# One transformer layer with retrieved experts: gate products copied by ScalarE and multiplied in by GpSimd

## The chip, the core and the metric

One core of a Trainium2 chip. The metric is the device time of one execution in microseconds, the median of three runs. The engines are named as in the profile: PE is TensorE (matmuls; PEld its weight loads), DVE is VectorE, ACT is ScalarE, POOL is GpSimd, SP is SyncE, which only issues transfers here.

## What is computed

One encoder layer on 512 tokens of width 1024 in float32. Its first half (a projection, a gating group, a retention group, an output projection, a layer norm) is not touched. Its second half retrieves experts:

```
q = h @ w_q;  scores = q . sub_keys             # 8 heads, 2 x 128 keys
top_s, top_i = top_k(scores, 16)                # per half of the query
cand = top_s[0][:, None] + top_s[1][None, :]    # 256 pairs, expert = i0 * 128 + i1
best, expert_idx = top_k(cand, 16);  gates = softmax(best)
act = gelu(h . u_tab[expert_idx])               # 128 experts a token
ffn = sum(gates * act * v_tab[expert_idx])
out = layer_norm(2 ** 0.25 * h + ffn)
```

## The kernel before

The 512 tokens are four tiles of 128. Tiles 0 and 1 are *gathered*: for each of 256 rows (16 units of a tile and a head, 16 experts each) GpSimd issues an indirect DMA for a row of `u_tab` and, 32 rows later (`LAG`), one for the row of `v_tab`; VectorE forms the dot product (`product_row`, L916) and adds the weighted row to the tile's sum (`add_row`, L937). Each kind has a ring of six buffers, so a gather waits until VectorE has used the row six before. VectorE's program is one loop over n = 0 to 287, in which the choices of later units (`choose_gathered`, `choose_dense`) stand at fixed rows.

Tiles 2 and 3 are *dense*: all 16384 experts are computed for their 256 tokens by TensorE, in two rounds of 64 blocks of 128 experts. A round has three parts in TensorE's order (`static_jobs`): `act`, products with 64 blocks of `u_tab`, whose GELU ScalarE writes to `X` (partitions are experts of a block, 64 blocks x 256 tokens); `gate`, which turns the chosen indices into dense weights; `expert`, products of the weighted `X` with 64 blocks of `v_tab`, accumulated in PSUM banks 0 to 3. SyncE loads the 256 blocks in this order into a ring of eight buffers (`load_block`, L440); block b waits until block b - 8 is used.

The gate part has 32 groups (`GROUPS`) of 8 tokens a round. For each, VectorE compares the tokens' second and first key indices with a grid, which gives one-hots in bf16 (`eqi`, L953, for 64 of the first keys; `ohj`, L954, for the 128 second keys), multiplies the first by the gates split in three bf16 pieces (`ohi`, L959), and TensorE multiplies the two (24 matmuls, L1264) into a PSUM bank of 8 tokens x 64 blocks. VectorE then multiplies that bank into `X` (`dense_weights`, L982) for the group before the one whose one-hots it just made. `ohi` has one buffer, `ohj` two. The banks rotate over four. The rounds stand in VectorE's loop in front of row 70 and row 190, with all 32 groups at once; TensorE's experts wait for `s_wgtd`, which VectorE signals at a round's end.

Tile 0's last norm (`finish`, `layer_norm`, L671 to L679) stands at row 160; its weights `lnp2` lie over the scores of tile 0 and are loaded by SyncE between block 127 and block 128, once eight units are chosen. Tile 1's norm follows row 287, then those of the dense tiles. SBUF is nearly full: `S` (first 8192 columns of `pool_mem`) holds the scores of all tiles, 2048 columns each, and `X` covers the rest and the scores of the dense tiles.

Of the kernel before, what the change touches and what calls it, by code (L numbers as in the profile page):

```python
# [5 lines left out]
P = 128  # L6
# [5 lines left out]
PH, TOPK, NK = 8, 16, 128  # L12
RING = 6
# [4 lines left out]
HALF = NK // 2  # L18
# [5 lines left out]
ROUND_ROW = (70, 190)  # L24
PER_ROW = 32

# [28 lines left out]
def static_jobs():  # L55
# [6 lines left out]
    def add(kind, *arg, by):  # L62
        jobs.append((kind, arg, by))
# [87 lines left out]
    for r in range(2):  # L151
        for n in range(HALF // 2):
            add("act", r, n, by="act")
            if (r, n) in during:
                jobs.append(("gelu", (during[r, n],), None))
            if (r, n) == (0, 28):
                jobs.append(("gates", (), None))
        if r == 0:
            add("selT", 0, by="act")
            add("selT", 1, by="act")  # L160
        for n in range(GROUPS):
            add("gate", r, n, by="dve")
            if (r, n) in within:
                jobs.append(("gelu", (within[r, n],), None))
        for u in range(4, 7) if r == 0 else range(10, GUNITS):
            jobs.append(("gelu", (u,), None))
        for n in range(HALF):
            jobs.append(("expert", (r, n), None))
# [29 lines left out]
def layer(nc, x, w_in, sgu_ln_w, sgu_ln_b, sgu_w_s, sgu_b, decay_fwd, decay_bwd, gn_w, w_out, ln1_w, ln1_b,  # L198
# [12 lines left out]
    with ctx:  # L211
# [48 lines left out]
        X = pool_mem[:, 4096:20480].rearrange("p (i n) -> p i n", i=HALF)  # L260
        lnp2 = S[:, 0:2048].rearrange("p (a n) -> p a n", a=2)
        S4 = S.rearrange("p (t q n) -> p t q n", t=NT, q=2 * PH)
# [26 lines left out]
        lookd = y[:, 3072:4096].bitcast(bf16)  # L289
        ohi = sb("ohi", [P, 2, 3, HALF, 4], bf16)  # L290
        grid = sb("grid", [P, NK, 4], bf16)
        table = sb("table", [P, TOPK, TOPK], bf16)
        work = sb("work", [P, 512])
        lookg = work[:, 0:256].bitcast(bf16)
        eqi = work[:, 256:512].bitcast(bf16).rearrange("p (q n t) -> p q n t", q=2, t=4)
        ident = sb("ident", [P, P])
# [64 lines left out]
        s_oh = sem("onehots_ready")  # L361
        s_act, s_wgtd = sem("dense_gelu_ready"), sem("dense_weights_ready")
        s_vdone = sem("experts_added")
# [18 lines left out]
        def _(sp):  # L382
# [58 lines left out]

            for b in range(2 * HALF):
                load_block(b)
            sp.wait_ge(s_best, PH)
            sp.dma_start(lnp2[:, 0, :], ln2_w[0].partition_broadcast(P)).then_inc(s_ln, 16)
            sp.dma_start(lnp2[:, 1, :], ln2_b[0].partition_broadcast(P)).then_inc(s_ln, 16)
            for b in range(2 * HALF, 4 * HALF):
                load_block(b)
# [9 lines left out]
        def _(pool):  # L458
# [36 lines left out]
            def gather_v(n):  # L495
# [3 lines left out]
                if n >= RING:  # L499
# [3 lines left out]
                                             ).then_inc(s_v[n % RING], 16)  # L503

            for n in range(ROWS + LAG):
                if n < ROWS:
                    gather_u(n)
                if n >= LAG:
                    gather_v(n - LAG)
# [3 lines left out]
        def _(act):  # L513
# [12 lines left out]
            for kind, arg, by, b, n in JOBS:  # L526
# [93 lines left out]
                elif kind == "selT":  # L620
                    a = arg[0]
                    copy(selT[:, 0:2, a * P:(a + 1) * P], bank4[:, 0:2, :])
                    copy(gateT[0][:, a * P:(a + 1) * P], bank4[:, 2, :]).then_inc(free[b], 1)
                    A.drain().then_inc(s_selT, 1)

            for t in range(GATHERED):
# [7 lines left out]
        def _(dve):  # L634
# [294 lines left out]
            def add_row(n):  # L929
# [9 lines left out]
                fence()  # L939

            def gate_rows(r, n):

                g = r * GROUPS + n
                t0 = 8 * n

                def spread(row, width):
                    return selT[:, row, t0:t0 + 8].rearrange("p (q t) -> p q t", q=2).unsqueeze(2).broadcast_to(
                        [P, 2, width, 4])

                def both(part, width):  # L950
                    return part.unsqueeze(1).broadcast_to([P, 2, width, 4])

                V.tensor_tensor(eqi, spread(0, HALF), both(grid[:, r * HALF:(r + 1) * HALF, :], HALF), ALU.is_equal)  # L953
                V.tensor_tensor(ohj[:, g % 2], spread(1, NK), both(grid[:], NK), ALU.is_equal)  # L954
                fence()
                if g:
                    b, used_ = BANK["gate", (g - 1) // GROUPS, (g - 1) % GROUPS]
                    dve.wait_ge(full[b], used_ + 1)
                V.tensor_tensor(ohi[:].rearrange("p q c n t -> p q c (n t)"),  # L959
                                eqi.rearrange("p q n t -> p q (n t)").unsqueeze(2).broadcast_to([P, 2, 3, HALF * 4]),  # L960
                                pieces[:, 2 * n:2 * n + 2].rearrange("p q c t -> p (q c) t").unsqueeze(2).broadcast_to(
                                    [P, 6, HALF, 4]), ALU.mult)
                fence().then_inc(s_oh, 1)  # L963

            def gate_pieces():

                for c in range(3):
# [6 lines left out]
                    fence()  # L974

            def dense_weights(r, n):
                b, used_ = BANK["gate", r, n]
                dve.wait_ge(full[b], used_ + 1)
                if n == 0:
                    dve.wait_ge(s_act, r + 1)  # L980
                x3 = X[:, :, 8 * n:8 * n + 8]
                V.tensor_tensor(x3, ps[:, b, :].rearrange("p (t i) -> p i t", t=8), x3, ALU.mult).then_inc(free[b], 1)  # L982

# [22 lines left out]
            for n in range(ROWS + LAG):  # L1006
# [9 lines left out]
                for r in range(2):  # L1016
                    if n == ROUND_ROW[0] and r == 0:
                        dve.wait_ge(s_selT, 2)
                        gate_pieces()
                    if 0 <= n - ROUND_ROW[r] < GROUPS // PER_ROW:  # L1020
                        first = (n - ROUND_ROW[r]) * PER_ROW
                        for g in range(first, first + PER_ROW):
                            gate_rows(r, g)
                            if g:
                                dense_weights(r, g - 1)
                        if first + PER_ROW == GROUPS:
                            dense_weights(r, GROUPS - 1)
                            fence().then_inc(s_wgtd, 1)  # L1028
                if n < ROWS:
                    product_row(n)  # L1030
                if n >= LAG:
                    add_row(n - LAG)
                if n == PH * TOPK + LAG:
                    dve.wait_ge(s_ln, 64)
                    finish(acc_rows[0]).then_inc(s_ln2, 1)
                    fence()
# [15 lines left out]
        def _(pe):  # L1052
# [43 lines left out]
            for kind, arg, by, b, n in JOBS:  # L1096
                if kind in ("split", "norm", "scale", "gelu", "gates"):
                    continue
                if kind == "expert":
                    r, i = arg  # L1100
                    if i == 0:
                        pe.wait_ge(s_wgtd, r + 1)
                    if i == 0 and r == 0:
# [154 lines left out]
                elif kind == "gate":  # L1258
# [3 lines left out]
                    for t in range(8):  # L1262
                        for c in range(3):
                            last = T.matmul(bank[:, t * HALF:(t + 1) * HALF], ohj[:, g % 2, t // 4, :, t % 4],  # L1264
                                            ohi[:, t // 4, c, :, t % 4],
                                            start=(c == 0), stop=(c == 2))
# [43 lines left out]
```

## Time and profile before

| | us |
|---|---|
| median of three runs (1617.83 to 1618.03) | 1617.87 |
| the profiled execution, its own time | 1619.71 |
| its span in the profile | 1617.6 |

| engine | busy, us | share of the span |
|---|---|---|
| TensorE matmul | 1398.0 | 86% |
| VectorE | 1226.6 | 76% |
| GpSimd | 631.8 | 39% |
| ScalarE | 175.1 | 11% |

A row of the profile names the line of the kernel, the engine, the operation and what it writes and reads, `out<-in`. "Idle before" is the time in which the engine stood still just before it, with what ended that wait. Busy shares are means over stages with different limits; the stages are, in order: the first half of the layer to about 240 us, queries and scores to 390, then round 0 (acts, gates, experts) and round 1 (the same), with the gathered rows beside them, and a tail of gathered rows and norms.

### The profile page before, as it was taken

To read this page: it belongs to the slowest core of one execution; us is meant where nothing else is said; L and a number is where in the kernel's file an instruction comes from. 1 tells how busy PE (TensorE), PEld (TensorE's weight loads), DVE (VectorE), ACT (ScalarE), POOL (GpSimd) and SP (SyncE) were. 2 spreads that over 40 slices of the span, in tenths; PEclk is the share of its full clock that TensorE was granted. 3 is DMA by queue.
4 is the path that set the end of the run, shared out by engine and by line. 5 is a ranking of instruction groups with operands and counts; after the bars stand their busy time and mean duration, and the time that the engine had idled before them with its cause. 6 is when DMAs were issued, how large, how long until landed. Compare 5 with 4: busy or idle time off the path is not lost.

```text
span 1617.6 us, 18280 instructions
## 1 busy us (share of the span) xinstructions
PE 1398.0 (86%) x6410; PEld 964.5 (60%) x6410; DVE 1226.6 (76%) x2527; ACT 175.1 (11%) x272; POOL 631.8 (39%) x548
## 2 busy tenths in 40 slices
PE   8999989999999999558999999999995599999600
PEld 6787655888777777454444457777775544444200
DVE  5745527788889883899867758778878987856888
ACT  4223001112110102000000001101011000000000
POOL 2243101222334262004636455664660046544671
PEclk9999999999999999557999999999995589999855
DMA  6320513465988799005999999999992069999993
GB/s 233 119 89 16 208 52 130 157 203 208 387 316 304 286 369 343 4 1 218 409 409 409 409 409 409 409 409 380 410 409 116 1 244 409 410 409 409 410 329 131
DMA packets 136714, 444.24 MB, mean 275 GB/s; under 512 B 13616, under 2 KB 26416, under 8 KB 136624
## 3 DMA queue, kind: packets, MB, share of 16 engines
q0 software_dynamic: 73728, 268.47, 42.9%
q1 hardware_dynamic: 62320, 173.56, 28.4%
q8 instruction: 51, 0.84, 0.2%
q10 hardware_dynamic: 576, 1.05, 0.2%
q14 instruction: 39, 0.32, 0.1%
HBM read 440.93 MB, written 2.10 MB: 274 GB/s over the span
## 4 chain that ended last, share of the span: by engine, by line
PE 40%; DMA 25%; DVE 17%; POOL 9%; issue 6%; DVEq 2%; ACT 1%; ACTq 0%; SPq 0%; POOLq 0%
PE ps L1057 23%; DMA big<-in_peer_v_dram,idx 22%; PE ps L1264 7%; PE ps L1074 6%; POOL big L501 5%; POOL big L491 4%; DVE ohi L959 4%; DVE y L937 3%; DMA big<-in_peer_u_dram,idx 2%; DVE big L916 2%; PE ps L1215 1%; PE ps L1242 1%; PE ps L1196 1%; DVE nw L661 1%; PE ps L1170 1%
## 5 line engine op out<-in xcount | busy, mean ns | idle before, releaser
L491 POOL DMA_INDIRECT big<-in_peer_u_dram,idx x256 | 289.0, 1129 | 683.5 <-DVE dots L916 565.0
L916 DVE CUSTOM_DVE_ANT_0 big<-big,xh 128x1024 f32<-128x1024 f32 x256 | 312.0, 1225 | 92.2 <-DMA big<-in_peer_u_dram,idx 73.5
L937 DVE SCALAR_TENSOR_TENSOR y<-big,wgt,y 128x1024 f32<-128x1024 f32 x256 | 328.5, 1283 | 69.0 <-DMA big<-in_peer_v_dram,idx 65.9
L501 POOL DMA_INDIRECT big<-in_peer_v_dram,idx x256 | 281.8, 1101 | 129.9 <-DVE y L937 69.2
L1057 PE MATMUL ps<-xT,big 128*128 128x256 f32 x1024 | 237.1, 385 | 10.8 <-issue 8.3
L1057 PEld LDWEIGHTS ps<-xT,big 128*128 128x128 f32 x1024 | 189.5, 190 | 58.5 <-issue 35.5
L1109 PE MATMUL ps<-big,pool_mem 128*128 128x512 f32 x512 | 222.3, 592 | 0.0
L1264 PE MATMUL ps<-ohi,y 128*128 128x64 bf16 x1536 | 105.7, 242 | 80.0 <-DVEq L963 80.0
L1109 PEld LDWEIGHTS ps<-big,pool_mem 128*128 128x128 f32 x512 | 97.4, 190 | 122.3 <-issue 122.3
L1264 PEld LDWEIGHTS ps<-ohi,y 128*128 128x128 bf16 x1536 | 96.5, 125 | 89.4 <-issue 89.4
L1057 PE MATMUL ps<-xT 128*128 128x256 f32 x512 | 118.5, 385 | 5.4 <-issue 4.1
L1109 PE MATMUL ps<-xT,pool_mem 128*128 128x512 f32 x256 | 112.5, 592 | 0.0
L1057 PEld LDWEIGHTS ps<-xT 128*128 128x128 f32 x512 | 94.7, 190 | 29.2 <-issue 17.7
L1057 PE MATMUL ps<-xT,pool_mem 128*128 128x256 f32 (+1 forms) x512 | 101.5, 358 | 1.8 <-ACTq L588 1.5
L1057 PEld LDWEIGHTS ps<-xT,pool_mem 128*128 128x128 f32 x512 | 87.3, 193 | 12.0 <-issue 2.4
L616 ACT ACTIVATE pool_mem<-ps 128x512 f32<-128x512 f32 x64 | 38.2, 597 | 498.3 <-PE ps L1057 498.3
L1109 PEld LDWEIGHTS ps<-xT,pool_mem 128*128 128x128 f32 x256 | 48.7, 190 | 61.2 <-issue 61.2
L1074 PE MATMUL ps<-weight_parts,x_hi 128*128 128x512 f32 x320 | 82.8, 404 | 0.8 <-ACT weight_parts L517 0.8
L375 POOL TENSOR_TENSOR weight_parts<-big,weight_parts 128x1024 fp32r<-128x1024 f32 x20 | 49.0, 2473 | 84.4 <-ACT weight_parts L517 84.4
L1074 PEld LDWEIGHTS ps<-weight_parts,x_hi 128*128 128x128 f32 x320 | 59.8, 191 | 14.7 <-ACT weight_parts L517 2.4
L959 DVE TENSOR_TENSOR ohi<-work,pieces 128x1536 bf16<-128x1536 bf16 x64 | 61.3, 958 | 9.4 <-PE ps L1264 2.3
L1109 PE MATMUL ps<-wr,pool_mem 128*128 128x512 f32 x128 | 61.7, 628 | 1.7 <-DVEq L1028 1.7
(193 smaller groups left out, 1425.3 us busy)
## 6 DMA issues: line engine op xcount, KB each, us to landing
big<-u_blocks_dram SPq DMA_DIRECT2D x64, 512.0 KB, 7.0
big<-in_peer_v_dram SPq DMA_DIRECT2D x64, 512.0 KB, 6.8
xT<-u_blocks_dram SPq DMA_DIRECT2D x32, 512.0 KB, 6.8
xT<-in_peer_v_dram SPq DMA_DIRECT2D x32, 512.0 KB, 6.8
big<-in_w_in_dram SPq DMA_DIRECT2D x24, 512.0 KB, 5.7
pool_mem<-in_peer_w_q_dram SPq DMA_DIRECT2D x12, 1024.0 KB, 5.5
wr<-u_blocks_dram SPq DMA_DIRECT2D x16, 512.0 KB, 6.9
y<-u_blocks_dram SPq DMA_DIRECT2D x16, 512.0 KB, 6.8
```

The source lines that it names most:

```text
L375: return engine.tensor_tensor(w_lo(g)[:, ks, :], w_full(g)[:, ks, :], w_hi(g)[:, ks, :].bitcast(f32), ALU.subtract)
L491: nc.gpsimd.indirect_dma_start(urow[n % RING], None, peer_u2, bass.IndirectOffsetOnAxis(ap=idx[:, u, e:e + 1], axis=0)).then_inc(s_u[n % R ...
L501: nc.gpsimd.indirect_dma_start(vrow[n % RING], None, peer_v2, bass.IndirectOffsetOnAxis(ap=idx[:, u, e:e + 1], axis=0)).then_inc(s_v[n % R ...
L616: A.activation(X[:, i:i + 2, :], bank.rearrange("p (i n) -> p i n", i=2), ACT.Gelu).then_inc(free[b], 1)
L661: V.scalar_tensor_tensor(r, a, 1.5, r, ALU.add, ALU.mult)
L916: V.tensor_tensor_reduce(out=urow[n % RING], in0=urow[n % RING], in1=xh[:, u // PH * D:(u // PH + 1) * D], scale=1.0, scalar=0.0, op0=ALU. ...
L937: V.scalar_tensor_tensor(acc_rows[t], vrow[n % RING], wgt[:, u % 2, e:e + 1], acc_rows[t], ALU.mult, ALU.add).then_inc(s_vadd, 1)
L959: V.tensor_tensor(ohi[:].rearrange("p q c n t -> p q c (n t)"), eqi.rearrange("p q n t -> p q (n t)").unsqueeze(2).broadcast_to([P, 2, 3, ...
L1057: last = T.matmul(dst, lhs(i), rhs(i), start=(i == 0), stop=(i == n - 1))
L1074: last = T.matmul(dst, *((a, b_) if x_left else (b_, a)), start=(n == 0 and k == 0), stop=(n == 2 and k == KC - 1))
L1109: last = T.matmul(acc[a][:, half * 512:(half + 1) * 512], X[:, i, a * P:(a + 1) * P], rows_v[:, half * 512:(half + 1) * 512], start=(r == ...
L1264: last = T.matmul(bank[:, t * HALF:(t + 1) * HALF], ohj[:, g % 2, t // 4, :, t % 4], ohi[:, t // 4, c, :, t % 4], start=(c == 0), stop=(c ...
```

## The change

- A gate job's bank is now read by ScalarE, which copies it with its two inner axes exchanged into `gbuf` (two buffers of 512 columns in tile 0's part of `S`), frees the bank and signals `s_gbuf`. From the third copy on it waits for the product two before.
- GpSimd multiplies `gbuf` into `X` (`dense_weights`, now in GpSimd's program, 32 at once in front of its gathers n = 76 and n = 196) and signals `s_prod`, for which TensorE's experts now wait.
- VectorE no longer multiplies. It makes `eqi` one group ahead (`first_key`, two buffers), `ohi` has a second buffer, and it waits for the matmuls of the group before last instead of the last; the drain between `ohj` and `ohi` is gone.
- `lnp2` moves to tile 1's part of `S`. Its two loads stand in front of block 240 and wait for all 16 units' choices; tile 0's norm stands at row 240.

```
--- before.py
+++ after.py
@@ -22,7 +22,8 @@
-PER_ROW = 32
+LN2_BLOCK = 240
+FINISH0 = 240
...
@@ -159,7 +160,7 @@
-            add("gate", r, n, by="dve")
+            add("gate", r, n, by="act")
...
@@ -258,7 +259,8 @@
-        lnp2 = S[:, 0:2048].rearrange("p (a n) -> p a n", a=2)
+        gbuf = [S[:, 512 * k:512 * k + 512].rearrange("p (i t) -> p i t", t=8) for k in range(2)]
+        lnp2 = S[:, 2048:4096].rearrange("p (a n) -> p a n", a=2)
...
@@ -287,12 +289,14 @@
-        ohi = sb("ohi", [P, 2, 3, HALF, 4], bf16)
+        ohi = [half.bitcast(bf16).rearrange("p (q c n t) -> p q c n t", q=2, c=3, t=4)
+               for half in (sb("ohi", [P, 768])[:, :], S[:, 1024:1792])]
...
-        eqi = work[:, 256:512].bitcast(bf16).rearrange("p (q n t) -> p q n t", q=2, t=4)
+        eqi = [work[:, 256 * k:256 * k + 256].bitcast(bf16).rearrange("p (q n t) -> p q n t", q=2, t=4)
+               for k in range(2)]
...
@@ -439,12 +443,12 @@
-            for b in range(2 * HALF):
+            for b in range(LN2_BLOCK):
                 load_block(b)
-            sp.wait_ge(s_best, PH)
+            sp.wait_ge(s_best, GUNITS)
             sp.dma_start(lnp2[:, 0, :], ln2_w[0].partition_broadcast(P)).then_inc(s_ln, 16)
             sp.dma_start(lnp2[:, 1, :], ln2_b[0].partition_broadcast(P)).then_inc(s_ln, 16)
-            for b in range(2 * HALF, 4 * HALF):
+            for b in range(LN2_BLOCK, 4 * HALF):
                 load_block(b)
...
@@ -502,7 +506,19 @@
+            def dense_weights(r):
+
+                pool.wait_ge(s_act, r + 1)
+                for n in range(GROUPS):
+                    g = r * GROUPS + n
+                    pool.wait_ge(s_gbuf, g + 1)
+                    x3 = X[:, :, 8 * n:8 * n + 8]
+                    nc.gpsimd.tensor_tensor(x3, gbuf[g % 2], x3, ALU.mult).then_inc(s_prod, 1)
+
             for n in range(ROWS + LAG):
+                for r in range(2):
+                    if n == ROUND_ROW[r] + RING:
+                        dense_weights(r)
                 if n < ROWS:
                     gather_u(n)
...
@@ -622,6 +638,13 @@
+                elif kind == "gate":
+                    r, n_ = arg
+                    g = r * GROUPS + n_
+                    if g >= 2:
+                        act.wait_ge(s_prod, g - 1)
+                    copy(gbuf[g % 2], bank.rearrange("p (t i) -> p i t", t=8)).then_inc(free[b], 1)
+                    A.drain().then_inc(s_gbuf, 1)
...
@@ -938,26 +961,30 @@
+            def first_key(r, n):
+
+                V.tensor_tensor(eqi[n % 2], spread(0, n, HALF), both(grid[:, r * HALF:(r + 1) * HALF, :], HALF),
+                                ALU.is_equal)
+
             def gate_rows(r, n):
 
                 g = r * GROUPS + n
...
-                V.tensor_tensor(eqi, spread(0, HALF), both(grid[:, r * HALF:(r + 1) * HALF, :], HALF), ALU.is_equal)
-                V.tensor_tensor(ohj[:, g % 2], spread(1, NK), both(grid[:], NK), ALU.is_equal)
-                fence()
-                if g:
-                    b, used_ = BANK["gate", (g - 1) // GROUPS, (g - 1) % GROUPS]
+                if n + 1 < GROUPS:
+                    first_key(r, n + 1)
+                if g >= 2:
+                    b, used_ = BANK["gate", (g - 2) // GROUPS, (g - 2) % GROUPS]
                     dve.wait_ge(full[b], used_ + 1)
-                V.tensor_tensor(ohi[:].rearrange("p q c n t -> p q c (n t)"),
-                                eqi.rearrange("p q n t -> p q (n t)").unsqueeze(2).broadcast_to([P, 2, 3, HALF * 4]),
+                V.tensor_tensor(ohj[:, g % 2], spread(1, n, NK), both(grid[:], NK), ALU.is_equal)
+                V.tensor_tensor(ohi[g % 2].rearrange("p q c n t -> p q c (n t)"),
+                                eqi[n % 2].rearrange("p q n t -> p q (n t)").unsqueeze(2).broadcast_to(
+                                    [P, 2, 3, HALF * 4]),
                                 pieces[:, 2 * n:2 * n + 2].rearrange("p q c t -> p (q c) t").unsqueeze(2).broadcast_to(
                                     [P, 6, HALF, 4]), ALU.mult)
                 fence().then_inc(s_oh, 1)
...
@@ -972,14 +999,6 @@
-            def dense_weights(r, n):
-                b, used_ = BANK["gate", r, n]
-                dve.wait_ge(full[b], used_ + 1)
-                if n == 0:
-                    dve.wait_ge(s_act, r + 1)
-                x3 = X[:, :, 8 * n:8 * n + 8]
-                V.tensor_tensor(x3, ps[:, b, :].rearrange("p (t i) -> p i t", t=8), x3, ALU.mult).then_inc(free[b], 1)
...
@@ -1017,20 +1036,16 @@
-                    if 0 <= n - ROUND_ROW[r] < GROUPS // PER_ROW:
-                        first = (n - ROUND_ROW[r]) * PER_ROW
-                        for g in range(first, first + PER_ROW):
+                    if n == ROUND_ROW[r]:
+                        first_key(r, 0)
+                        fence()
+                        for g in range(GROUPS):
                             gate_rows(r, g)
-                            if g:
-                                dense_weights(r, g - 1)
-                        if first + PER_ROW == GROUPS:
-                            dense_weights(r, GROUPS - 1)
-                            fence().then_inc(s_wgtd, 1)
                 if n < ROWS:
                     product_row(n)
                 if n >= LAG:
                     add_row(n - LAG)
-                if n == PH * TOPK + LAG:
+                if n == FINISH0:
                     dve.wait_ge(s_ln, 64)
                     finish(acc_rows[0]).then_inc(s_ln2, 1)
                     fence()
...
@@ -1099,7 +1114,7 @@
                     if i == 0:
-                        pe.wait_ge(s_wgtd, r + 1)
+                        pe.wait_ge(s_prod, GROUPS * (r + 1))
...
@@ -1262,7 +1277,7 @@
                             last = T.matmul(bank[:, t * HALF:(t + 1) * HALF], ohj[:, g % 2, t // 4, :, t % 4],
-                                            ohi[:, t // 4, c, :, t % 4],
+                                            ohi[g % 2][:, t // 4, c, :, t % 4],
```

## Rows read from the trace of the kernel before

**Rows 1.** Page: the chain's shares by engine; the DMA rate in 40 slices.
```profile
PE 40%; DMA 25%; DVE 17%; POOL 9%; issue 6%; DVEq 2%; ACT 1%; ACTq 0%; SPq 0%; POOLq 0%
GB/s 233 119 89 16 208 52 130 157 203 208 387 316 304 286 369 343 4 1 218 409 409 409 409 409 409 409 409 380 410 409 116 1 244 409 410 409 409 410 329 131
```

**Rows 2.** Windows: stretch, length, busy of PE, PEld, DVE, ACT, POOL, PEclk, DMA share, GB/s.
```profile
1250.00:1300.00 50.00, 29.01 (x424) 26.42 (x421) 45.73 (x71) 0.00 (x0) 0.00 (x0) 0.50 0.00 1
...
1460.00:1500.00 40.00, 40.00 (x95) 17.71 (x94) 24.93 (x29) 3.18 (x5) 18.52 (x20) 1.00 1.03 409
...
1510.00:1524.00 14.00, 14.00 (x34) 5.95 (x32) 13.21 (x17) 0.00 (x0) 10.65 (x12) 1.00 1.03 410
```

**Rows 3.** Timeline, one step of round 0: start, us, engine, line, tiles [idle before].
```profile
658.22 0.96 DVE L959 TENSOR_TENSOR ohi<-work,pieces 128x1536 bf16<-128x1536 bf16 x1
659.29 0.69 DVE L982 TENSOR_TENSOR pool_mem<-ps,pool_mem 128x512 f32<-128x512 f32 x1
...
659.35 1.66 PE L1264 MATMUL ps<-ohi,y 128*128 128x64 bf16 x24 [1.17 <-DVEq L963]
659.90 0.41 DVE L953 TENSOR_TENSOR work<-selT,grid 128x512 bf16<-128x512 bf16 x1
660.23 0.68 DVE L954 TENSOR_TENSOR y<-selT,grid 128x1024 bf16<-128x1024 bf16 x1
661.05 0.96 DVE L959 TENSOR_TENSOR ohi<-work,pieces 128x1536 bf16<-128x1536 bf16 x1
```

**Rows 4.** Timeline, 148 to 151 us: a ScalarE copy, GpSimd, VectorE beside it.
```profile
148.56 0.60 ACT L580 ACTIVATE pool_mem<-ps 128x512 f32<-128x512 f32 x1 [3.94 <-PE ps L1074]
149.34 1.27 POOL L477 TENSOR_TENSOR pool_mem<-pool_mem 128x512 f32<-128x512 f32 x1 [13.35 <-ACTq L581]
149.42 0.69 DVE L798 SCALAR_TENSOR_TENSOR big<-ps,y 128x512 f32<-128x512 f32 x1 [5.33 <-PE ps L1170]
```

**Rows 5.** Timeline, VectorE beside GpSimd's multiplications, and the same forms alone.
```profile
30.29 2.28 DVE L726 TENSOR_TENSOR dec<-dec 128x8 f32<-128x8 f32 x1
...
54.64 2.81 DVE L677 SCALAR_TENSOR_TENSOR pool_mem<-pool_mem,mv 128x512 f32<-128x512 f32 x1
57.52 0.75 DVE L679 SCALAR_TENSOR_TENSOR pool_mem<-pool_mem,nw 128x512 f32<-128x512 f32 x1
...
118.87 0.17 DVE L694 TENSOR_TENSOR dec<-dec 128x8 f32<-128x8 f32 x1
...
124.90 2.40 POOL L375 TENSOR_TENSOR weight_parts<-big,weight_parts 128x1024 fp32r<-128x1024 f32 x1 [7.83 <-ACT weight_parts L517]
127.87 3.12 DVE L715 SCALAR_TENSOR_TENSOR y<-pool_mem,dec,y 128x896 f32<-128x896 f32 x1
...
137.80 1.15 DVE L715 SCALAR_TENSOR_TENSOR y<-pool_mem,dec,y 128x896 f32<-128x896 f32 x1
...
198.81 1.53 DVE L987 CAST grid<-iota 128x512 bf16<-128x512 f32 x1
```

**Rows 6.** Timeline, end of round 0 and begin of round 1.
```profile
738.74 1.64 PE L1264 MATMUL ps<-ohi,y 128*128 128x64 bf16 x24 [1.17 <-DVEq L963]
741.21 6.08 PE L1109 MATMUL ps<-wr,pool_mem 128*128 128x512 f32 x8 [0.83 <-DVEq L1028]
742.78 1.74 POOL L491 DMA_INDIRECT big<-in_peer_u_dram,idx  x1 [108.43 <-DVE dots L916]
...
1212.30 1.64 PE L1264 MATMUL ps<-ohi,y 128*128 128x64 bf16 x24 [1.31 <-DVEq L963]
```

**Rows 7.** Landing of L445 and L446; timeline: row 241; tile 1's norm, first, last.
```profile
DMA to landing us min/median/max: 10.2/11.3/12.3
...
1502.91 1.23 DVE L916 CUSTOM_DVE_ANT_0 big<-big,xh 128x1024 f32<-128x1024 f32 x1 [0.95 <-DMA big<-in_peer_u_dram,idx]
...
1590.68 1.29 DVE L671 BATCH_NORM_STATS2 st<-y 128x6 f32<-128x512 f32 x2
...
1596.99 0.75 DVE L679 SCALAR_TENSOR_TENSOR y<-y,nw,pool_mem 128x512 f32<-128x512 f32 x1
```

More of the change, by code:

```diff
@@ L361, in layer @@
         s_oh = sem("onehots_ready")
-        s_act, s_wgtd = sem("dense_gelu_ready"), sem("dense_weights_ready")
+        s_act, s_gbuf, s_prod = sem("dense_gelu_ready"), sem("gate_products_copied"), sem("dense_weights_ready")
         s_vdone = sem("experts_added")
@@ L939, in add_row, with both, spread @@
                 fence()
+            def both(part, width):
+                return part.unsqueeze(1).broadcast_to([P, 2, width, 4])
+            def spread(row, n, width):
+                return selT[:, row, 8 * n:8 * n + 8].rearrange("p (q t) -> p q t", q=2).unsqueeze(2).broadcast_to(
+                    [P, 2, width, 4])
+            def first_key(r, n):
+                V.tensor_tensor(eqi[n % 2], spread(0, n, HALF), both(grid[:, r * HALF:(r + 1) * HALF, :], HALF),
+                                ALU.is_equal)
             def gate_rows(r, n):
                 g = r * GROUPS + n
[L944 to L951, printed above, removed]
-                V.tensor_tensor(eqi, spread(0, HALF), both(grid[:, r * HALF:(r + 1) * HALF, :], HALF), ALU.is_equal)
-                V.tensor_tensor(ohj[:, g % 2], spread(1, NK), both(grid[:], NK), ALU.is_equal)
-                fence()
-                if g:
-                    b, used_ = BANK["gate", (g - 1) // GROUPS, (g - 1) % GROUPS]
+                if n + 1 < GROUPS:
+                    first_key(r, n + 1)
+                if g >= 2:
+                    b, used_ = BANK["gate", (g - 2) // GROUPS, (g - 2) % GROUPS]
                     dve.wait_ge(full[b], used_ + 1)
-                V.tensor_tensor(ohi[:].rearrange("p q c n t -> p q c (n t)"),
-                                eqi.rearrange("p q n t -> p q (n t)").unsqueeze(2).broadcast_to([P, 2, 3, HALF * 4]),
+                V.tensor_tensor(ohj[:, g % 2], spread(1, n, NK), both(grid[:], NK), ALU.is_equal)
+                V.tensor_tensor(ohi[g % 2].rearrange("p q c n t -> p q c (n t)"),
+                                eqi[n % 2].rearrange("p q n t -> p q (n t)").unsqueeze(2).broadcast_to(
+                                    [P, 2, 3, HALF * 4]),
                                 pieces[:, 2 * n:2 * n + 2].rearrange("p q c t -> p (q c) t").unsqueeze(2).broadcast_to(
```

## Prediction

> **What bounds the kernel now.** I read the chain of work that ended last first. It names TensorE, the DMA of gathered rows, VectorE and GpSimd in turn [rows 1], so no engine is the limit everywhere, and the question is which one ends each stage. The slices show two holes in the DMA traffic [rows 1]. These are the two gate rounds, 32 groups each, about 646 to 741 us and 1210 to 1302 us. The table of windows shows what such a stretch is like and what the others are like: inside round 1 the DMA queues carry nothing, the granted clock is 0.50 and VectorE is busy 91% of the time. In the expert phase the DMA is saturated at 409 GB/s, TensorE is busy without a gap and VectorE waits. In the last stretch before TensorE ends, VectorE is busy 13.21 of 14 us [rows 2].
>
> One step of a gate round is in [rows 3]. VectorE makes the first one-hot (0.42 us), the second (0.68), the gated one (0.96), then multiplies a finished gate out of PSUM (0.69). The gated one-hot starts at 658.22 and again at 661.05, so a step takes 2.83 us, and nothing on that engine waits. TensorE needs 1.66 us of each step and idles for the rest, waiting for the one-hots. A round is therefore VectorE's serial time, and nothing else advances in it. Each microsecond per step is 64 us of the kernel.
>
> **The step without its multiplication.** By starts in [rows 3], first to second one-hot is 0.33 us, second to gated 0.82, gated to multiplication 1.07, multiplication to the next first one-hot 0.61. The change removes the last interval. It also takes away the drain between second and gated one-hot: there 0.60 remains (0.68 less the 0.08 that consecutive instructions overlap). Sum: 0.33 + 0.60 + 1.07 = 2.00 us. TensorE still needs 1.66 us plus the 0.17 us from the end of the gated one-hot to its first matmul [rows 3], so 1.83, under 2.00. With two gated buffers its wait for the group before last is past. ScalarE copies 128x512 out of PSUM in 0.60 us, and GpSimd starts 0.78 us after such a copy starts [rows 4]. The reads here are strided by 64 elements; VectorE reads this layout in the 0.69 us that it also takes for a straight one [rows 3, 4], so I take no surcharge and bound it at twice the copy, which would still be under a step. GpSimd multiplies 128x512 by 128x512 in 1.27 us [rows 4]. So each of the four engines alone would fit in 2.00 us.
>
> **What GpSimd's multiplication does to VectorE.** Three rows decide this. A VectorE instruction of 8 elements with two SBUF inputs takes 0.17 us alone, and 2.28 us when it begins under a GpSimd multiplication. A cast to bf16 of 512 elements takes 1.53 us beside GpSimd's. Yet one that reads PSUM and only one SBUF tensor takes its usual 0.69 us in the middle of GpSimd's 1.27 [rows 4, 5]. The multiplication that is removed was of the last kind; the three one-hot instructions that stay read two SBUF tensors each. The price comes from a stretch in which both engines had work queued: VectorE's instruction of line 715, 1.15 us alone, took 3.12 us there, so the 1024-wide GpSimd operation, 2.40 us long, put 1.97 us into VectorE's sequence: its length less 0.43 [rows 5]. For 512 elements this gives 1.27 - 0.43 = 0.84 us. A second place shows a smaller overlap: a 512-wide instruction, 0.75 us alone, took 2.81 us, so 2.06 us were put in, the length less 0.34 [rows 5]; that gives 0.93. I take 0.90. Bounds: nothing (step 2.00) and the whole 1.27 (step 3.27). I stay near 0.90 since both direct rows lie there.
>
> The step then is 2.00 + 0.90 = 2.90 us against 2.83: the gain of 0.83 is eaten and 0.07 us is lost. Does GpSimd come at the cheap place? A product is ready 0.17 + 1.66 + 0.04 + 0.78 = 2.65 us after the end of its gated one-hot; the next gated one-hot runs from 1.94 to 2.90 on that scale. So GpSimd waits for its end and takes the gap at the drain, as in the priced stretch. If it came between the second and the gated one-hot, which have no drain between them, it would put in some 0.2 us more per step, 13 us in all.
>
> The Trainium skill (SBUF — State Buffer, Who interferes with whom) says that a VectorE instruction with two SBUF inputs contends with a GpSimd instruction that reads SBUF, that the two share ports under an exclusive lock, and that the loser is blocked for the whole instruction. The trace agrees on who is blocked (2.28 against 0.17 us), but not quite on the amount: by the page the step would be the plain sum 3.27 us and the kernel some 24 us slower than by my step, which I keep as an end of the range.
>
> **The edges of the rounds.** Entry to round 0 is set by TensorE and ScalarE; the first group now makes one more first one-hot and a drain before TensorE can start: 0.4 us. In each round the first step has no GpSimd product yet (-0.9) and the second product may fall at the dearer place (+0.2). So round 0 costs VectorE 0.4 + 31 x 0.07 - 0.7 = 1.9 us. At its end, TensorE started the experts 0.83 us after its last gate matmul [rows 6]. Now ScalarE (0.04 + 0.78) and GpSimd (1.27) and a semaphore (0.1) stand there: 2.2 us, or up to 3.4 where VectorE's next row instruction, which also reads two SBUF tensors (1.23 us [rows 7]), goes first. That is 1.4 to 2.6; I take 2.0. TensorE leaves round 0 3.9 us late and works without a gap up to round 1. There it had waited 1.31 us for the first one-hots [rows 6]. VectorE reaches that point earlier relative to it now, since a norm and two loads have left the stretch (below), so 1.2 of it are given back: round 1 starts 2.7 us late. It takes +1.5, rows start again with two products still to go on GpSimd, in front of its gathers: before, the first gather was issued 742.78, 2.4 us after TensorE's last gate (740.38) [rows 6], now some 3.3: +0.9, partly covered by the six rows that lie ready. I book 0.5. Rows run 4.7 us late.
>
> On ScalarE the gelus of the next units now stand behind the copies; they are first needed two rows after a round, 5 us away, and I cost them at nothing. GpSimd's gathers behind the products wait for rows that VectorE has not yet used, so they lose only the 0.5 above.
>
> **The late norm.** The tile-0 norm takes 7.1 us of VectorE (1590.68 to 1597.74 for the same work on tile 1 [rows 7]). At row 160 it lay in the saturated stretch, where VectorE waits for rows. At row 240 it lies at about 1502 us: the row before it came with 0.95 us of waiting [rows 7], the ones after 1506 with none, VectorE being 94% busy [rows 2]. So little absorbs it: 1.3 us of row waits directly, up to 3 if the saturated stretch lasts longer because TensorE is late. Cost 4 to 6; I take 5. If all were absorbed it would be nothing, at worst 7.1.
>
> The two loads of the norm's weights (0.5 MB each into 128 partitions) move from before round 1, where TensorE sets the end, to before block 240, where the row chain is short of bandwidth: 1.05 MB / 409 GB/s = 2.6 us [rows 2]. They landed within 12.3 us of issue [rows 7]. On SyncE's queue they now wait for unit 15's choice, made at row 210; SyncE reaches block 240 when expert 40 of round 1 is used, at about 1303 + 40 x 3.4 = 1439 us (95 matmul records in 40 us [rows 2], 8 to a block). Row 210 comes at about 1382 (row 190 at 1303, row 241 at 1502.91 [rows 7]: 3.9 us each). So that wait is past, eight blocks are loaded ahead, and row 240 comes 50 us after the loads. No stall.
>
> **Sum.** 4.7 + 2.6 + 5 = 12.3 us on a span of 1617.6. The profiled execution took 1619.71 us, 2.1 around the span; the median is 1617.87, so the profile is 0.1% slow and the difference carries over. 1617.9 + 12.3 = 1630 us.
>
> **Rivals.** (a) GpSimd does not block the bf16 one-hots (no row shows bf16 instructions with two inputs beside it). Then a step is 2.00 us: 1630 less 62 x 0.90 = 1574. For it: only that the exact form is unseen. Against it: every two-input row beside GpSimd, and the bf16 cast. 11%. (b) Partial blocking, 0.2 to 0.7 us per step: 1587 to 1618. 9%. (c) The other side, and my forecast: the products put 0.8 to 1.1 us into each step: 1624 to 1642. It decides from 0.70 us per step on, where 62 x (0.83 - 0.70) = 8 us of gain just pay for the other 8 us of the sum (edges, loads and norm, 12.3 - 62 x 0.07). 65%. (d) GpSimd's product is dearer than 1.27, because it reads and writes runs of 8 elements 1 KB apart, or nothing overlaps: 3.1 to 3.6 us a step, 1642 to 1673. Its straight and its 128-element-run forms differ by nothing that matters; runs of 8 are unseen. 15%.
>
> **How the numbers follow.** About 0.2% (3 us) is what a measurement of this kernel tells from no change. Likeliest: (c), 1630. Its own range is 1624 to 1642. The range to 8 in 10 takes (c), the upper half of (b) and most of (d): 1602 to 1655. Slower by over 0.2%: (c) nearly whole, (d): 0.79. Same: the edge between (b) and (c), 0.04. Faster: 0.17.
>
> **What would show it.** In the profile after: the distance of successive gated one-hots, 2.9 us (2.0 means (a)); the mean of VectorE's bf16 instructions in a round, one of the three longer by 0.9 to 1.2 us per step; GpSimd's 64 products at 1.3 to 2.2 us; TensorE waiting about 1.2 us per step for one-hots at clock 0.50; the norm at row 240 and no row waits after it; experts starting 2.2 to 3.4 us after the last gate matmul. I am wrong if the bf16 forms run at 0.42, 0.68 and 0.96 beside GpSimd, or if the product's layout is slow.

## The result, and the profile after

| | before, us | after, us |
|---|---|---|
| median (4 runs each) | 1617.95 | 1629.19 |
| lowest to highest | 1617.83 to 1621.08 | 1627.99 to 1630.44 |
| profiled execution: its time, its span | 1619.71, 1617.6 | 1629.49, 1627.7 |

The changed kernel is slower, by a ratio of 1.0065 (95% interval 1.005 to 1.0079). The forecast was 1630, with "slower by over 0.2%" at 0.79.

Timeline of the changed kernel, one step of round 0 and the start of the next (start, us, engine, line, tiles, idle before); it answers [rows 3]. L973 is the first one-hot, L984 the second, L985 the gated one, L533 ScalarE's copy, L516 GpSimd's product:

```profile
658.96 1.31 DVE L973 TENSOR_TENSOR work<-selT,grid 128x512 bf16<-128x512 bf16 x1
659.02 1.65 PE L1279 MATMUL ps<-pool_mem,y 128*128 128x64 bf16 x24 [1.26 <-DVEq L990]
660.20 0.68 DVE L984 TENSOR_TENSOR y<-selT,grid 128x1024 bf16<-128x1024 bf16 x1
660.71 0.60 ACT L533 ACTIVATE pool_mem<-ps 128x512 f32<-128x512 f32 x1 [2.32 <-PE ps L1279]
660.80 0.94 DVE L985 TENSOR_TENSOR ohi<-work,pieces 128x1536 bf16<-128x1536 bf16 x1
661.42 1.48 POOL L516 TENSOR_TENSOR pool_mem<-pool_mem 128x512 f32<-128x512 f32 x1 [1.43 <-ACTq L647]
661.86 1.31 DVE L973 TENSOR_TENSOR work<-selT,grid 128x512 bf16<-128x512 bf16 x1
```

The first one-hot starts at 658.96 and at 661.86: a step is 2.90 us, where 2.83 was before. The multiplication is gone from VectorE, and the first one-hot, 0.42 us before, takes 1.31. It begins 0.11 us after the gated one-hot ends and lasts to 663.17, 0.27 us past the end of GpSimd's product at 662.90. GpSimd's own row begins at 661.42, under the gated one-hot, which is not lengthened: there GpSimd is the one that waits. TensorE works 1.65 us and waits 1.26.

Windows of the changed kernel, busy us of PE, PEld, DVE, ACT, POOL, then granted clock, DMA share, GB/s; they answer [rows 2]:

```profile
1250.00:1300.00 50.00, 28.34 (x413) 25.74 (x410) 47.98 (x53) 10.42 (x18) 25.31 (x17) 0.50 0.01 1
1460.00:1500.00 40.00, 40.00 (x94) 17.68 (x93) 22.89 (x28) 0.00 (x0) 16.86 (x18) 1.00 1.03 409
```

In the round ScalarE and GpSimd now work too, yet VectorE's busy time rose from 45.73 to 47.98 of 50 us, because blocked time counts as busy. The granted clock is 0.50 in both kernels, the lower of TensorE's two levels (1.2 GHz). In the saturated stretch TensorE is busy without a gap and the DMA at 409 GB/s, as before.

**Where the 10.1 us of span came from.** By starts of the same instruction in the two timelines (after less before):

| instruction | shift, us |
|---|---|
| gated one-hot of group 0, round 0 | +0.15 |
| gated one-hot of group 31, round 0 | +1.3 |
| first expert matmul, round 0 | +3.4 |
| first gate matmul, round 1 | +2.4 |
| gated one-hot of group 31, round 1 | +3.4 |
| row 190, row 192 | +0.8, +2.7 |
| row 240 (both weight loads lie in front) | +5.7 |
| row 241 (the norm lies in front) | +12.3 |
| last added row, its end; end of the span | +10.1 |

### The profile page after: what moved, and what is told of

Its sections match the earlier page's. It is cut to its first block, busy times and chain, and to the rows that moved or that the text cites. A ratio compares the mean times of both kernels' runs of the same rounds, so it can differ in the third digit from the quotient of the medians.

```text
span 1627.7 us, 18406 instructions
## 1 busy us (share of the span) xinstructions
PE 1398.6 (86%) x6410; PEld 964.6 (59%) x6410; DVE 1241.4 (76%) x2463; ACT 213.4 (13%) x336; POOL 738.4 (45%) x612
## 4 chain that ended last, share of the span: by engine, by line
PE 62%; DVE 17%; DMA 8%; issue 4%; POOL 4%; DVEq 4%; ACT 1%; ACTq 0%; SPq 0%
PE ps L1072 37%; PE ps L1124 14%; DMA big<-in_peer_v_dram,idx 8%; PE ps L1089 6%; DVE work L973 5%; POOL big L505 3%; DVEq L990 2%; DVE y L960 2%; DVE big L939 2%; DVE pool_mem L985 2%; DVE ohi L985 2%; POOL big L495 1%; PE ps L1230 1%; PE ps L1257 1%; PE ps L1211 1%
## 5 line engine op out<-in xcount | busy, mean ns | idle before, releaser
L939 DVE CUSTOM_DVE_ANT_0 big<-big,xh 128x1024 f32<-128x1024 f32 x256 | 315.8, 1240 | 80.9 <-DMA big<-in_peer_u_dram,idx 62.5
L505 POOL DMA_INDIRECT big<-in_peer_v_dram,idx x256 | 289.4, 1130 | 132.9 <-DVE y L960 73.3
L1072 PE MATMUL ps<-xT,big 128*128 128x256 f32 x1024 | 237.1, 385 | 10.9 <-issue 8.3
L516 POOL TENSOR_TENSOR pool_mem<-pool_mem 128x512 f32<-128x512 f32 x64 | 97.2, 1519 | 112.0 <-ACTq L647 112.0
L533 ACT ACTIVATE pool_mem<-ps 128x512 f32<-128x512 f32 (+2 forms) x116 | 66.7, 575 | 332.1 <-PE ps L1279 148.6
L1279 PE MATMUL ps<-ohi,y 128*128 128x64 bf16 x768 | 52.9, 242 | 41.9 <-DVEq L990 41.6
L1279 PE MATMUL ps<-pool_mem,y 128*128 128x64 bf16 x768 | 52.8, 242 | 39.7 <-DVEq L990 39.7
L973 DVE TENSOR_TENSOR work<-selT,grid 128x512 bf16<-128x512 bf16 x64 | 75.3, 1177 | 7.5
```

The lines of the kernel that those rows point to most:

```text
L505: nc.gpsimd.indirect_dma_start(vrow[n % RING], None, peer_v2, bass.IndirectOffsetOnAxis(ap=idx[:, u, e:e + 1], axis=0)).then_inc(s_v[n % R ...
L516: nc.gpsimd.tensor_tensor(x3, gbuf[g % 2], x3, ALU.mult).then_inc(s_prod, 1)
L533: return A.activation(dst, src, ACT.Copy)
L939: V.tensor_tensor_reduce(out=urow[n % RING], in0=urow[n % RING], in1=xh[:, u // PH * D:(u // PH + 1) * D], scale=1.0, scalar=0.0, op0=ALU. ...
L973: V.tensor_tensor(eqi[n % 2], spread(0, n, HALF), both(grid[:, r * HALF:(r + 1) * HALF, :], HALF), ALU.is_equal)
L1072: last = T.matmul(dst, lhs(i), rhs(i), start=(i == 0), stop=(i == n - 1))
```

## The experiments

e1 to e9 ran on three chips (e1, e4, e5 and e6 on one, e2, e3, e7 and e9 on a second, e8 on a third), and on all three the kernel before took 1705 to 1738 us. In the traces of these runs TensorE waits for its blocks, which it does not in the trace of before (see e8 below). The expectations speak of one chip; that is not so. Of these runs only the lengths of steps and local distances are read, except where the text says so. e10 and e11 ran on a fourth chip and e12 on a fifth, where the kernel before took 1618.9 and 1619.5. Times are medians; e2, e3, e6, e7 and e11 are single executions.

**Is it GpSimd's access that lengthens the step?** e3 replaces the read and multiply by a write, e7 by a copy (one input), e2 halves the product.

```
-  nc.gpsimd.tensor_tensor(x3, gbuf[g % 2], x3, ALU.mult).then_inc(s_prod, 1)
+  nc.gpsimd.memset(x3, 0.5).then_inc(s_prod, 1)               # e3
+  nc.gpsimd.tensor_copy(x3, gbuf[g % 2]).then_inc(s_prod, 1)  # e7
+  # e2: x3 and gbuf cut to [:, 0:HALF // 2, :], else as before
```

> The changed kernel with GpSimd writing a constant to the same slice of X in place of the product: it waits and signals as before and writes SBUF, but reads nothing from it; the gates have no effect on the output. If VectorE's two-input instructions are blocked only by GpSimd's reads: a step of 2.00 us, the bf16 instructions at 0.42, 0.68 and 0.96 us, time 1629 - 62 x 0.90 - 2 = 1571. If any SBUF access of GpSimd blocks them: 2.0 plus the memset's length less 0.37, so 2.1 to 2.4 us and 1577 to 1598.

> The changed kernel with GpSimd copying the gates into X in place of multiplying: it reads one SBUF operand and writes one; the activations have no effect on the output. If reads block: a step of 2.0 us plus the copy's length (I guess 0.6 to 0.9 us) less 0.37, so 2.2 to 2.5 us and 1584 to 1605. If only operations with two SBUF inputs on both sides collide: 2.00 us and 1571.

> The changed kernel with GpSimd multiplying only half of each product (128x256; the other 32 blocks of experts keep unweighted activations). Nothing else is changed. My theory (the step is VectorE's 2.00 us plus GpSimd's length less about 0.37): GpSimd's length falls from 1.27 to about 0.72 us, the step from 2.90 to 2.35, the time to 1629 - 62 x 0.55 = 1595. Rival (a fixed cost of each exchange between the engines): the step stays at 2.9, the time at 1629.

| run | GpSimd's op, us | step, us (median) | VectorE's three, us |
|---|---|---|---|
| e3, memset | 0.53 | 2.02 | 0.43, 0.69, 0.95 |
| e7, copy | 0.62 to 0.91 | 2.44 | 0.43, 1.10, 0.95 or 0.88, 0.68, 0.95 |
| e2, half a product | 0.74 | 2.52 | 0.92, 0.68, 0.94 |
| after | 1.31 alone, 1.48 with its wait | 2.90 | 1.31, 0.68, 0.94 |

Their totals, 1682.35 us (e3), 1703.97 (e7) and 1704.13 (e2) against a single 1737.99 of the kernel before, lie far from the forecasts of 1571 to 1605, and so does the kernel before from its 1618; they are not used. Timeline of e3, one step:

```profile
689.66 0.69 DVE L984 TENSOR_TENSOR y<-selT,grid 128x1024 bf16<-128x1024 bf16 x1
689.74 0.53 POOL L516 MEMSET pool_mem<- 128x512 f32 x1 [1.49 <-ACTq L647]
690.26 0.95 DVE L985 TENSOR_TENSOR ohi<-work,pieces 128x1536 bf16<-128x1536 bf16 x1
691.33 0.43 DVE L973 TENSOR_TENSOR work<-selT,grid 128x512 bf16<-128x512 bf16 x1
691.38 1.65 PE L1279 MATMUL ps<-ohi,y 128*128 128x64 bf16 x24 [0.36 <-DVEq L990]
```

GpSimd writes SBUF in the middle of the second one-hot, and that takes its usual 0.69. In 59 of the 64 memsets the second one-hot is the one beside it, so the other two forms are not tested for more than 0.01 us of overlap. The waits, semaphores and copies are those of the changed kernel, so neither the handshakes nor ScalarE sets the step: what is left is 2.02, the 2.00 of the prediction. Timeline of e7:

```profile
690.15 0.95 DVE L985 TENSOR_TENSOR ohi<-work,pieces 128x1536 bf16<-128x1536 bf16 x1
691.20 0.62 POOL L516 COPY pool_mem<-pool_mem 128x512 f32<-128x512 f32 x1 [1.51 <-ACTq L647]
691.22 0.88 DVE L973 TENSOR_TENSOR work<-selT,grid 128x512 bf16<-128x512 bf16 x1
692.02 0.68 DVE L984 TENSOR_TENSOR y<-selT,grid 128x1024 bf16<-128x1024 bf16 x1
```

One read operand on GpSimd's side is enough to hold VectorE. That is what the Trainium skill (SBUF — State Buffer, Who interferes with whom) states for a VectorE instruction with two SBUF inputs: contention with a GpSimd instruction that reads SBUF, none with one that only writes. Both halves of the sentence hold here, 2.44 against 2.02 us a step.

e2 lies at 2.52, not at the 2.35 I expected. Its timeline shows why:

```profile
690.04 0.94 DVE L985 TENSOR_TENSOR pool_mem<-work,pieces 128x1536 bf16<-128x1536 bf16 x1
691.03 0.74 POOL L516 TENSOR_TENSOR pool_mem<-pool_mem 128x256 f32<-128x256 f32 x1 [1.79 <-ACTq L647]
691.10 0.95 DVE L973 TENSOR_TENSOR work<-selT,grid 128x512 bf16<-128x512 bf16 x1
```

The product comes 0.05 us after the gated one-hot's end (690.98), and it puts in 0.52 us, its length less 0.22. The copy of e7, which also arrives there, puts in 0.42 of its 0.62, its length less 0.20. "Length less 0.4" holds where GpSimd was already waiting; I take the other 0.2 for its start-up, then hidden behind VectorE's work, which no run separates. The full product put in 0.88 to 0.90 by steps of 2.90 against 2.02 or 2.00.

**Is it the copy or who multiplies?** e4 gives the product back to VectorE, out of PSUM, and keeps the new one-hots; e6 keeps ScalarE's copy as well and lets VectorE multiply from it.

```
...
                         for g in range(GROUPS):
                             gate_rows(r, g)
+                            if g:
+                                dense_weights(r, g - 1)
+                        dense_weights(r, GROUPS - 1)
+                        fence().then_inc(s_prod, GROUPS)
...
```

> The changed kernel with the product given back to VectorE, which again multiplies the bank in PSUM into X; no copy on ScalarE, nothing on GpSimd in the rounds. The one-hots stay as changed: first one-hot one group ahead, two gated buffers, one drain less. My theory: a step is 0.33 + 0.60 + 1.07 + 0.61 = 2.61 us against 2.90 with GpSimd and 2.83 before, so 1629 less 62 x 0.29 = 18 us, less 2 to 4 us at the rounds' ends: 1607 to 1610. Rival (the step is bound by the exchange between one-hots and matmuls, and not by what stands on VectorE): a step stays at 2.8 to 2.9 us and the time at 1625 to 1630.

> The changed kernel with ScalarE's copy kept, but VectorE and not GpSimd multiplies the copy into X. VectorE then has four instructions a step with two SBUF inputs each, and GpSimd does nothing beside them. My theory (GpSimd's operation blocks VectorE, the copy costs nothing): a step of 2.6 us, 1608 to 1611. Rival (the detour over ScalarE and its handshakes set the step): 2.9 us and 1629.

The steps: 2.61 us in e4 and 2.62 in e6, both as expected. Timeline of e4:

```profile
692.70 0.69 DVE L990 TENSOR_TENSOR pool_mem<-ps,pool_mem 128x512 f32<-128x512 f32 x1
692.75 1.65 PE L1272 MATMUL ps<-ohi,y 128*128 128x64 bf16 x24 [0.96 <-DVEq L971]
693.31 0.41 DVE L954 TENSOR_TENSOR work<-selT,grid 128x512 bf16<-128x512 bf16 x1
693.64 0.68 DVE L965 TENSOR_TENSOR y<-selT,grid 128x1024 bf16<-128x1024 bf16 x1
694.24 0.95 DVE L966 TENSOR_TENSOR pool_mem<-work,pieces 128x1536 bf16<-128x1536 bf16 x1
695.31 0.69 DVE L990 TENSOR_TENSOR pool_mem<-ps,pool_mem 128x512 f32<-128x512 f32 x1
```

The detour over ScalarE adds 0.01 us to a step; the new one-hots (the first made one group ahead, a second gated buffer, one drain less) together are worth 0.22 us a step (2.83 to 2.61), and no run separates the three. On VectorE the product costs 0.61 us of the step, on GpSimd 0.90. The part of the change that looked like preparation was the gain, and the part that gave it its name was the loss. The totals missed the forecasts of 1607 to 1611: 1719.9 in e4 and 1723.6 in e6. e4 was even slower than the kernel before on its chip (ratio 1.0073, 1.0042 to 1.0104). TensorE waited for blocks there, and e12 below gives a total where it did not.

**The late norm.** e1 and e9 are the kernel before with only the late norm and its late loads; e5 is e4 with both earlier.

```
+LN2_BLOCK = 240     # e5, e8, e12: 226
+FINISH0 = 240       # e5, e8, e12: 218
...
-        lnp2 = S[:, 0:2048]...
+        lnp2 = S[:, 2048:4096]...
...
```

> The kernel before with only the last norm's part of the change: weights behind the scores of tile 1, loaded in front of block 240, tile 0's norm at row 240. Everything in the gate rounds stays as it was. My theory: the two loads cost the row chain 2.6 to 3 us and the norm 4 to 6 us of a VectorE that no longer waits for rows, about 1 us is given back in front of round 1: 1618 + 6 to 7 = 1624 to 1625. Rival: the norm is hidden wherever it stands, and the whole loss of the change comes from the gate rounds: 1618.

> The kernel of e1 again (before, with only the norm and its loads late), for a chip where the kernel before takes 1618 us. My theory: 2.6 to 3 us of loads and 4 to 5 us of norm, 1 us given back before round 1: 1624 to 1625. Rival: hidden, 1618.

> The same as the run before it, with tile 0's norm at row 218 and its weights loaded in front of block 226. There VectorE still waits about 1.3 us a row for gathered rows and has 20 such rows to make good 7.1 us. My theory: 4 to 5 us faster than with the norm at row 240: 1603 to 1605. Rival: the norm's place does not matter: no difference.

e1 took 1676.0 us and e9 1692.2, on two chips where the kernel before took 1706.3 and 1706.8; both of my totals missed, and there the late norm was even faster (ratios 0.982, 0.972 to 0.992, and 0.991, 0.987 to 0.995). What the two show of the norm is local: from row 240 to row 241 there are 10.50 us in e1 and 10.35 in e9, as in the changed kernel (10.52), against 4.00 before. So 6.4 to 6.5 us of the norm's 7.1 reach the row chain at that place, with the rounds as before or as changed. e5 took 1713.4 us, e4 1719.9: 6 us apart, but with spreads of 9 to 14 us, so this pair does not settle it.

> The kernel of e5 again, since on the chip of the first seven runs the kernel before took 1706 us, TensorE waiting there for its block loads, so that only lengths of steps could be compared. Where the kernel before takes its 1618 us I expect by my theory: 31 x 0.22 x 2 = 14 us less in the rounds (steps of 2.61 us measured against 2.83), less about 1 at their ends, plus 2.6 to 3 us for the late loads: 1606 to 1608. Rival: what VectorE saves in the rounds is lost again to TensorE or the rows: 1616 to 1620.

e8 gave 1714.1 against 1705.0 (ratio 1.0036, 1.0001 to 1.007), although its steps of 2.61 us were in place. TensorE's waits in its trace, and in that of the kernel before:

```profile
PE ps L1065 <- issue: 109.6, 71, 16.6
```
```profile
PE ps L1057 <- issue: 16.5, 64, 0.3
```

The columns are us in all, times, longest. 16.5 us are short waits at the drains after each block; the other 93 us I read as waits for blocks. The DMA records bear this out. From 1000 to 1050 us, in the second act part, the same kernel moves about as much in e8 as in e12 (404 and 407 GB/s), but the queue of the blocks gets 66 GB/s of it in e8 and 135 in e12, and that of the gathered rows 338 and 272. VectorE gains nothing by its rows: in e8 it then stands 72.6 us in round 1, waiting for TensorE. In e1 and e9 the same TensorE waits are 59.6 and 57.6 us, in e4 and e5 103.7 and 108.3: these sums differ by more than the 10 us at issue. The kernel before has no trace on these chips, and why the two queues share so unevenly there, and why the waits are shorter in e1 and e9, stays open.

> The changed kernel itself on the chip of the experiments (kernel before: about 1706 us there). Step of a gate round: 2.90 us as on the first chip, GpSimd's products 1.3 to 1.5 us, VectorE's first one-hot about 1.3 us beside them; this is my theory and does not depend on how fast blocks arrive. The total there is open: if only rounds, norm and loads counted, 1706 + 11 = 1717; if TensorE's waits for blocks move with the rows' timing, as the late norm alone gave 1692 where 1713 was due, anything from 1690 to 1720.

> The kernel before, for its trace on the same chip. Step of 2.83 us as on the first chip. Theory for its 1706 us: TensorE waits for block loads in the act phases, some 40 to 60 us in each, where on the first chip it waited for none (16.5 us of drains only). Rival: the whole machine is slower there (clock, matmuls, VectorE): then the step would be longer by 5% too.

These two did not land on one of the slower chips, so the question they were for (the traces of both kernels there) stays open; only the rival of a slower machine is out, since the steps of e1 and e9 are 2.82 us. They are a repetition: 1628.19 us against 1618.85, ratio 1.0055 (1.0033 to 1.0077), and steps of 2.91 and 2.82 us. TensorE's wait before the experts is 2.94 against 0.83, the distance of rows 192 and 240 grows by 3.2 us and that of rows 240 and 241 by 7.0. The absolute shifts are not the same: row 190 comes 2.4 us earlier than in e11, where it came 0.8 later in the first pair, and the spans differ by 7.9 us in place of 10.1. So a place in one trace is known to some 2 to 3 us.

> The kernel of e5 (product on VectorE, changed one-hots, norm at row 218), once more for a chip on which the kernel before takes 1618 us. My theory, from steps of 2.61 us measured: 1606 to 1608, faster than both kernels. Rival: the saving of the rounds is lost again behind them: 1616 to 1620.

e12: 1604.68 us (1604.39 to 1605.58) against 1619.53, ratio 0.9907 (0.9891 to 0.9924). It beats both kernels, by 15 us and, from another chip, by 24 us, and lies 1.3 us under the forecast. Its timeline at row 218:

```profile
1393.42 1.23 DVE L920 CUSTOM_DVE_ANT_0 big<-big,xh 128x1024 f32<-128x1024 f32 x1 [1.27 <-DMA big<-in_peer_u_dram,idx]
1395.98 1.28 DVE L941 SCALAR_TENSOR_TENSOR y<-big,wgt,y 128x1024 f32<-128x1024 f32 x1 [1.33 <-DMA big<-in_peer_v_dram,idx]
1397.36 1.29 DVE L675 BATCH_NORM_STATS2 st<-y 128x6 f32<-128x512 f32 x2
...
1404.56 1.23 DVE L920 CUSTOM_DVE_ANT_0 big<-big,xh 128x1024 f32<-128x1024 f32 x1
```

Row 219 follows row 218 by 11.1 us, as late as row 241 followed row 240. But here VectorE had been waiting 1.3 us before each instruction of a row, and after the norm it no longer waits (row 219 in the timeline), since the rings could fill meanwhile: rows 219 to 240 take 83.1 us where the kernel before took 87.5, and 240 to 255 another 1.1 less. Over rows 190 to 255 e12 is 3.2 us longer than before, about the price of the loads; the changed kernel is 11.0 longer.

## Why the prediction was right

**The step.** 2.00 + 0.90 = 2.90 us; measured 2.90, and e3 gives the 2.00 (2.02) alone. The rows that carried it were GpSimd's old multiplications with float32 VectorE instructions beside them [rows 5]; that bf16 forms are held in the same way, the gap on which rival (a) lived, is shown by the first one-hot's 1.31 us. Rival (b), 0.2 to 0.7 us a step, is out by the 0.90, and (d) by the step of 2.90: GpSimd's product takes 1.31 us where it does not wait, so runs of 8 elements 1 KB apart cost 0.04. The place was right too: GpSimd waits under the gated one-hot and takes the drain. The end that the Trainium skill's full exclusion gave (SBUF — State Buffer, Who interferes with whom), 3.27, is not met. The rows above show where VectorE does not lose 0.4 us of GpSimd's 1.31: 0.15 lie before the end of the gated one-hot (from 661.74 to 662.90 are 1.16), 0.12 in VectorE's own gap behind it, and 0.15 at the end, since the first one-hot takes 0.42 us alone and ends only 0.27 after the product.

**The edges: 4.7 us booked, 2.7 measured at row 192.** Round 0 cost VectorE 1.3 us in place of 1.9: the entry took 0.15 in place of 0.4, and I overlooked that the last group makes no first one-hot (0.33 us). TensorE's wait before the experts was 2.96 us in place of 0.83, so 2.1 against the 2.0 booked:

```profile
742.19 1.27 DVE L960 SCALAR_TENSOR_TENSOR y<-big,wgt,y 128x1024 f32<-128x1024 f32 x1
742.44 2.15 POOL L516 TENSOR_TENSOR pool_mem<-pool_mem 128x512 f32<-128x512 f32 x1 [1.25 <-ACTq L647]
743.61 2.07 DVE L939 CUSTOM_DVE_ANT_0 big<-big,xh 128x1024 f32<-128x1024 f32 x1
744.65 5.99 PE L1124 MATMUL ps<-wr,pool_mem 128*128 128x512 f32 x8 [2.96 <-POOL pool_mem L516]
```

The last product stands behind a row instruction and takes 2.15 us, and it holds the next one in turn: 2.07 in place of 1.23. These rows answer [rows 6]. The larger error is behind round 1, where I booked +0.5 for the rows. VectorE no longer waits for the last matmuls and a product of its own, which before took it 2.7 us after the last one-hot; it loses about 1.0 and 0.8 us to the last two products instead. The sign was wrong: -0.7.

**The loads: 2.6 booked, 3.0 measured** between row 192 and row 240. The traces of the kernel before alone differ by 1.5 us over this stretch (191.1, and 189.6 in e11), so the agreement is no proof of the price. No stall came of their new place: issued at 1448.3 and landed within 10.9 us, with row 240 at 1504.64.

**The norm: 5 booked.** 6.5 us at its place; 2.1 of it are given back behind row 241, 1.7 in the tail from row 255 to the last added row, so 4.4 stay. How much is given back and how much is scatter is open: the repetition shows 7.0 us at the place and a tail from row 255 of equal length in both kernels. No run has the changed rounds without the late norm where TensorE does not wait for blocks, so the parts of the total are distances in traces and not differences of runs.

So 2.7 + 3.0 + 6.5 - 2.1 = 10.1 us of span against 12.3 booked, and 11.2 in the medians. The step was sized rightly. The terms beside it miss by -2.0 (edges), +0.4 (loads) and -0.6 us (norm, itself +1.5 at its place and -2.1 behind it), so the sum is 2.2 us too high by the spans. That the forecast lies within 1 us of the median is luck in part: the medians differ by 1.1 us more than the spans, and the spans of the repetition by 7.9 only.

## What to carry to other kernels

Here the move to GpSimd ate the gain of the new one-hots (0.29 against 0.22 us a step), and by the distances above the late loads and norm make 7.4 of the 10.1 us lost. Before work is moved from VectorE to GpSimd, look at what stays on VectorE: if those instructions read two SBUF tensors each, and GpSimd's reads SBUF too, the two engines take turns: here an instruction that cost VectorE 0.61 us of its step out of PSUM cost it 0.90 when GpSimd did it. Find the price where the old trace has both engines at work at once, by how much an instruction is longer than alone, and ask whether the moved work will arrive before or within a VectorE instruction. A norm or any other block of VectorE time belongs where the profile shows that engine waiting for transfers, with enough rows behind it to catch up.

## What the runs showed of the hardware

GpSimd's write-only operation costs VectorE's two-input instruction beside it nothing (step 2.02 us with a 0.53 us memset beside the second one-hot), one with a single read holds such instructions (2.44). So for a constant GpSimd was free in this loop and for a copy it was not. And three chips ran the kernel before 5% slower than the others (1705 to 1707 us in the medians of several runs against 1618 to 1620) with gate steps of the same 2.82 us in e1 and e9. In e8, from there, the queue of the block loads got half of what it got in e12 (66 against 135 GB/s at a total of some 405), and kernels that differ by 1% came out in another order.
